# Order around seven norms rewritten, and two stages that scale their results by 1/rms instead of their inputs

## The chip, the cores and the metric

One Trainium2 chip, one of its cores. The metric is the device time of one launch, in microseconds (us), median over runs. TensorE multiplies (PE in the profile), VectorE (DVE), ScalarE (ACT) and GpSimd (POOL) do the elementwise work, SyncE (SP) starts the loads of weights. All five run at once and meet at semaphores.

## What is computed

A network of four layers on 512 tokens of width 1024, all in float32. The first half has two layers that end in layer norms, the second half two that use rms norms.

```
for layer in (0, 1):
    mix = hybrid_mixer(x) if layer == 0 else recurrent_mixer(x)
    x = layer_norm(DN_ALPHA * x + mix, ln1_g[layer], ln1_b[layer])
    x = layer_norm(DN_ALPHA * x + sqrelu_mlp(x, w1, w2), ln2_g[layer], ln2_b[layer])
h = x
for l in (0, 1):
    xn = rms_norm(h, g[0])
    mix = dilated_mixer(xn, w_qkv, w_o) if l == 0 else fox_mixer(xn, w_q, w_o, k, v, c)
    h = h + rms_norm(mix, g[1])
    h = h + rms_norm(conv_ffn(rms_norm(h, g[2]), w_up, conv, w_down), g[3])
rms_norm(x, g) = x * rsqrt(mean(x * x) + EPS) * g
```

`dilated_mixer` starts with q, k, v = xn @ w_qkv, then a rotation of q and k by position (rope) and banded attention. `fox_mixer` starts with q = xn @ w_q_b; its keys, values and gates come from rms_norm(h, kv_norm) @ w_kvf. So between every two matrix products stands a norm that needs a mean over the 1024 channels of each token before anything of the next product's input is final.

## The kernel before

Tokens lie along the free dimension (512), channels along the 128 partitions in 8 tiles (`X[:, m, :]`). A float32 product is done as three passes in a faster format: each operand is split in a high part and the rest (`XH`, `XL` for activations; `WH`, `WL` for weights), and `three` (L268 to L270) multiplies high by high, low by high and high by low. A **unit** is one 128-column block of a weight matrix times the whole input: 8 steps k of 3 matmuls, 24 in all. Unit u's weights are loaded to `RAW`, split by ScalarE (`split_hi`, L240) and VectorE (`split_lo`, L248), and lie in slot u % 4: a unit's weights can be split only when the unit four before it is done (`unit_done`).

Every engine runs its own list of instructions in the order in which the Python code issues it, and waits in it. That order is written by hand; the change rewrites it.

**At a norm** the tokens are worked in two halves, v = 0 and v = 1, of 256 columns. `last_four_pe` does the last four units of a stage, all of them for half 0 and then all for half 1, and between puts the two small matmuls of the statistics of half 0 (`stats_pe`, L443 for the sum and L447 for the sum of squares, with a matrix of 1/1024). `first_three_pe` does the first three units u0, u0+1, u0+2 of the next stage side by side, again half 0, then half 1: for each k it needs `XL[k]` of that half, and at k = 0 the split weights of the three. The statistics of half 1 go to TensorE behind its second step. The last four units occupy all four slots, so that the weights of u0 to u0+3 are split while the norm is computed. Meanwhile the others work per tile:

- layer norm: VectorE subtracts the mean (L498), GpSimd multiplies by 1/sigma (L512), ScalarE writes `XH` (L524) and `X` (L525) with gain and bias, VectorE writes `XL` (L504). `stats_end_act` and `stats_end_dve` turn the statistics into 1/sigma.
- rms norm of what is added (`rms_add_dve`): VectorE scales (L612) and adds (L615), GpSimd adds three of the eight tiles (L623), ScalarE writes `XH` (L651) and squares the new X (L539), GpSimd sums the squares (L553), VectorE writes `XL` (L642). Before the feed-forward stages 1/rms of the new X is applied to the results, since it is the same for all channels of a token.
- before the dilated and the query stage it is applied to the input: all squares of a half are summed, TensorE adds them over channels (`squares_pe`, L559), and only then VectorE writes x times gain times 1/rms (L582), ScalarE `XH` (L595) and VectorE `XL` (L587).

`lead_dve`, `lead_act` and `lead_pool` say between which tiles of half 0 the rest is done: results of half 1 taken from PSUM (`take`), its squares and sums (`stat`), and the splits of u0, u0+1 and u0+2, at tiles 3, 5 and 7.

There are eight such places: norms 0 to 2 (layer norms before `w1_0`, `rin`, `w1_1`), 3 (a layer norm and the rms norm before the dilated stage, `qkv`), 4 (`up_0`), 5 (the query stage, `wqb`), 6 (`up_1`) and 7 (the output).

Of the kernel before, what the change touches and what calls it, by code (L numbers as in the profile page):

```python
# [12 lines left out]
T = 512  # L13
# [120 lines left out]
def build_program(nc, D):  # L134
    with ExitStack() as ctx:
# [220 lines left out]
        HALF = (slice(0, 256), slice(256, 512))  # L356
        half_done = signal("half")
# [4 lines left out]
        def last_four_pe(pe, us, xh, xl, ready, taken, behind_first):  # L362

            kb = PLAN[us[4]][2]
            for v in range(2):
                for b, u in enumerate(us[4:8]):
                    claim(pe, b)
                    pe.wait_ge(w_lo, u)
                    for k in range(kb):
                        pe.wait_ge(*ready[k])  # L370
                        mm = three(pe, PS[b][:, HALF[v]], u, k, xh[k][:, HALF[v]], xl[k][:, HALF[v]], k == 0, k == kb - 1)
                    mm.then_inc(*(unit_done if v else half_done).at(u))
                    pe.until[b] = [taken(b + 4, v)]
                    if v and b == 0:
                        behind_first()
# [79 lines left out]
        def stats_end_act(act, n, v, mean):  # L455
# [6 lines left out]
            act.e.activation(S1[:, h], PS[b + 1][:, h], ACT.Square).then_inc(*st_m2.at((n, v)))  # L462
            act.wait_ge(st_var, (n, v))
            rstd_act(act, RS[:, h], S2[:, h], 1.0, EPS5, ("rstd", n, v)).then_inc(*st_r.at((n, v)))

        def stats_end_dve(dve, n, v):
# [9 lines left out]
              ("ln1", 1, ("rwo",), "mlp1"), ("ln2", 1, ("mlp", 1, 3), None)]  # L476
# [3 lines left out]
        BEFORE_STATS = {1: (st_r, (0, 1)), 2: (st_r, (1, 1)), 3: (st_r, (2, 1)), 4: (st_r, ("ln", 1)),  # L480
                        5: (st_r, (4, "x", 1)), 6: (st_r, (5, "x", 1)), 7: (st_r, (6, "x", 1))}
# [8 lines left out]

        def layer_norm_dve(dve, n, v, between):
            _, _, mix, stage = LN[n]
            h, b = HALF[v], 4 + 2 * v
            for i in range(10):
                if i < 8:
                    if i > 2:
                        dve.wait_ge(x_norm, (n, i - 3, v))
                    dve.e.tensor_tensor(TM[:, 3 + i % 3, h], X[:, i, h], PS[b + 1][:, h], ALU.subtract).then_inc(*ln_c.at((n, i, v)))  # L498
                m = i - 2
                if 0 < m and n == 3:  # L500
                    square_dve(dve, "ln", m, v)
# [13 lines left out]
        def layer_norm_act(act, n, v, between):  # L515
            name, l, _, stage = LN[n]
            h = HALF[v]
            for m in range(8):
# [7 lines left out]
                if n == 3:  # L526
                    act.wait_ge(x_norm, (n, m, v))
# [6 lines left out]
        def square_act(act, key, m, v):  # L534
            h, added = HALF[v], rs_sumd if key == "ln" else rs_sum
            if m > 2:
                act.wait_ge(added, (key, m - 2, v))
            out = TM[:, 6 + m % 2, h] if m else S1[:, h]
            act.e.activation(out, X[:, m, h], ACT.Square).then_inc(*rs_sq.at((key, m, v)))  # L539

        def square_dve(dve, key, m, v):
            h = HALF[v]
            dve.wait_ge(rs_sq, (key, m, v))
            if m > 1:
                dve.wait_ge(rs_sumd, (key, m - 1, v))
# [2549 lines left out]
```

## Time and profile before

| | |
|---|---|
| median of three runs | 2608.57 us (2605.19 to 2609.13) |
| profiled execution, own time | 2606.99 us |
| its span, first to last instruction | 2605.2 us |
| TensorE busy | 2457.0 us (94%) |
| VectorE busy | 1443.1 us (55%) |
| ScalarE busy | 1076.0 us (41%) |
| GpSimd busy | 304.1 us (12%) |
| granted clock of TensorE, mean | 0.969 |

The span is the time from the first to the last instruction in one profiled execution; 1.8 us lie around it. Busy shares are of the span. The granted clock is the share of TensorE's full speed; it takes two values, 1 and 0.5.

### The profile page before, as it was taken

To read this page: it belongs to the slowest core of one execution; us is meant where nothing else is said; L and a number is where in the kernel's file an instruction comes from. 1 tells how busy PE (TensorE), PEld (TensorE's weight loads), DVE (VectorE), ACT (ScalarE), POOL (GpSimd) and SP (SyncE) were. 2 spreads that over 40 slices of the span, in tenths; PEclk is the share of its full clock that TensorE was granted. 3 is DMA by queue.
4 is the path that set the end of the run, shared out by engine and by line. 5 is a ranking of instruction groups with operands and counts; after the bars stand their busy time and mean duration, and the time that the engine had idled before them with its cause. 6 is when DMAs were issued, how large, how long until landed. Compare 5 with 4: busy or idle time off the path is not lost.

```text
span 2605.2 us, 31632 instructions
## 1 busy us (share of the span) xinstructions
PE 2457.0 (94%) x12858; PEld 2029.9 (78%) x12858; DVE 1443.1 (55%) x2181; ACT 1076.0 (41%) x1878; POOL 304.1 (12%) x290
## 2 busy tenths in 40 slices
PE   8999989999989789999979979999979998999997
PEld 6768868888887688888857778888867777788886
DVE  6547755443366665334474467645475454676355
ACT  5533144232256554223254454433243555444332
POOL 0030130000031430000131021000020001101000
PEclk9989999999999899999989989999989999999998
DMA  5200012222213123222221123222212111232221
GB/s 196 89 33 1 17 43 88 101 93 97 97 50 113 65 76 103 97 97 97 81 78 57 41 69 110 97 97 94 84 64 91 33 49 50 81 109 86 98 100 45
DMA packets 56224, 206.47 MB, mean 79 GB/s; under 512 B 3680, under 2 KB 5776, under 8 KB 55952
## 3 DMA queue, kind: packets, MB, share of 16 engines
q1 hardware_dynamic: 55440, 201.34, 22.6%
q0 software_dynamic: 640, 3.12, 0.3%
q8 instruction: 102, 1.67, 0.3%
q14 instruction: 42, 0.34, 0.0%
HBM read 202.30 MB, written 2.10 MB: 78 GB/s over the span
## 4 chain that ended last, share of the span: by engine, by line
PE 80%; DVE 9%; issue 6%; ACT 4%; POOL 1%; DMA 0%; SPq 0%; POOLq 0%; DVEq 0%; ACTq 0%
PE ps L268 24%; PE ps L270 23%; PE ps L269 23%; DVE WL L248 2%; DVE TM L612 1%; ACT WH L240 1%; PE ps L317 1%; PE ps L2512 1%; PE ps L321 1%; PE ps L318 1%; PE ps L2541 1%; DVE X L615 1%; DVE AR L786 1%; DVE AR L1995 1%; DVE XL L642 1%
## 5 line engine op out<-in xcount | busy, mean ns | idle before, releaser
L268 PE MATMUL ps<-XH,WH 128*128 128x512 f32 (+1 forms) x2216 | 840.2, 379 | 92.2 <-DVE WL L248 39.3
L269 PE MATMUL ps<-XL,WH 128*128 128x512 f32 (+1 forms) x2216 | 819.2, 370 | 0.0
L270 PE MATMUL ps<-XH,WL 128*128 128x512 f32 (+1 forms) x2216 | 818.8, 369 | 0.0
L248 DVE TENSOR_TENSOR WL<-RAW,WH 128x1024 fp32r<-128x1024 f32 (+1 forms) x382 | 469.6, 1231 | 319.9 <-ACT WH L240 318.6
L268 PEld LDWEIGHTS ps<-XH,WH 128*128 128x128 f32 x2216 | 428.5, 193 | 181.4 <-issue 79.8
L240 ACT ACTIVATE WH<-RAW 128x1024 fp32r<-128x1024 f32 (+1 forms) x382 | 395.0, 1037 | 313.4 <-PE ps L270 305.7
L269 PEld LDWEIGHTS ps<-XL,WH 128*128 128x128 f32 x2216 | 428.9, 194 | 69.7 <-issue 4.6
L270 PEld LDWEIGHTS ps<-XH,WL 128*128 128x128 f32 x2216 | 427.9, 193 | 68.2
L268 PE MATMUL ps<-H,WH 128*128 128x512 f32 (+1 forms) x1104 | 405.5, 367 | 1.9 <-ACT AR L1903 1.9
L270 PE MATMUL ps<-H,WL 128*128 128x512 f32 (+1 forms) x1104 | 404.3, 366 | 0.0
L269 PE MATMUL ps<-H,WH 128*128 128x512 f32 (+1 forms) x1104 | 404.3, 366 | 0.0
L268 PEld LDWEIGHTS ps<-H,WH 128*128 128x128 f32 x1104 | 208.0, 188 | 40.2 <-DVE WL L248 2.3
L269 PEld LDWEIGHTS ps<-H,WH 128*128 128x128 f32 x1104 | 208.0, 188 | 37.6
L270 PEld LDWEIGHTS ps<-H,WL 128*128 128x128 f32 x1104 | 208.0, 188 | 37.4
L1176 ACT ACTIVATE TM<-TM,VEC 128x512 f32<-128x512 f32 x88 | 71.8, 816 | 209.1 <-DVE TM L1230 209.1
L1206 DVE SCALAR_TENSOR_TENSOR TM<-TM,VEC 128x511 f32<-128x511 f32 (+1 forms) x176 | 131.3, 746 | 3.1
L1273 POOL TENSOR_TENSOR TM<-TM 128x512 f32<-128x512 f32 x38 | 49.0, 1289 | 508.8 <-DVE TM L1206 468.1
L1075 DVE SCALAR_TENSOR_TENSOR TM<-ps,TM 128x512 f32<-128x512 f32 x64 | 44.2, 690 | 104.2 <-ACT TM L1054 104.2
L1054 ACT ACTIVATE TM<-ps 128x512 f32<-128x512 f32 x64 | 38.1, 595 | 136.9 <-PE ps L270 136.8
L1230 DVE TENSOR_TENSOR TM<-ps,TM 128x512 f32<-128x512 f32 x88 | 60.4, 687 | 40.1 <-PE ps L270 39.9
L623 POOL TENSOR_TENSOR X<-X,TM 128x256 f32<-128x256 f32 x24 | 23.2, 966 | 478.5 <-DVE TM L612 478.5
L420 DVE TENSOR_TENSOR TM<-TM 128x256 f32<-128x256 f32 (+1 forms) x88 | 55.5, 631 | 39.3 <-ACT TM L412 39.0
(369 smaller groups left out, 2535.6 us busy)
## 6 DMA issues: line engine op xcount, KB each, us to landing
RAW<-in_w SPq DMA_DIRECT2D x64, 1024.0 KB, 4.9
RAW<-in_up SPq DMA_DIRECT2D x44, 1024.0 KB, 4.9
RAW<-in_dn SPq DMA_DIRECT2D x16, 1024.0 KB, 4.9
RAW<-in_hyb SPq DMA_DIRECT2D x10, 1024.0 KB, 5.0
RAW<-in_qkv SPq DMA_DIRECT2D x9, 1024.0 KB, 4.8
RAW<-in_rin SPq DMA_DIRECT2D x8, 1024.0 KB, 4.8
RAW<-in_kvf SPq DMA_DIRECT2D x8, 1024.0 KB, 4.9
RAW<-in_dn SPq DMA_DIRECT2D x8, 768.0 KB, 4.4
```

The lines of the kernel that those rows point to most:

```text
L240: act.e.activation(WH[:, s, 0:n], RAW[:, g % NRAW, k, 0:n], ACT.Copy).then_inc(*w_hi.at(u))
L248: dve.e.tensor_tensor(WL[:, s, 0:n], RAW[:, g % NRAW, k, 0:n], f32(WH[:, s, 0:n]), ALU.subtract).then_inc(*w_lo.at(u))
L268: pe.e.matmul(out, wh, xh, start=first, stop=False)
L269: pe.e.matmul(out, wh, xl, start=False, stop=False)
L270: return pe.e.matmul(out, wl, xh, start=False, stop=last)
L420: dve.e.tensor_tensor(S2[:, c], S2[:, c], TM[:, 6 + m % 2, c], ALU.add).then_inc(*st_s2.at((n, m, v)))
L1054: act.e.activation(r, PS[m % 4][:, :], ACT.Relu).then_inc(*h_relu.at((l, q, m)))
L1075: dve.e.scalar_tensor_tensor(h, PS[m % 4][:, :], 0.0, r, ALU.max, ALU.mult).then_inc(*h_sq.at((l, q, m)))
L1176: act.e.activation(pair[s], TM[:, 6 + s, :], ACT.Identity, bias=vec("fcb", 44 * l + blk), scale=vec("fcw", 132 * l + 3 * blk + 2)).then_in ...
L1206: dve.e.scalar_tensor_tensor(dst[:, 2 - j:T], u[:, 0:T + j - 2], vec("fcw", 132 * l + 3 * blk + j), dst[:, 2 - j:T], ALU.mult, ALU.add).th ...
L1230: dve.e.tensor_tensor(TM[:, 6 + s, :], PS[b][:, :], RS, ALU.mult).then_inc(*f_u.at((l, q, m, s)))
L1273: pool.e.tensor_tensor(g, g, v, ALU.mult).then_inc(*gate_pool.at(("ffn", l, q, m)))
```

## The change

1. **The places in the order.** `lead_*` are gone. Each engine's list for half 0 is written out: results of half 1, weight splits and sums stand where their inputs are expected. ScalarE splits u0 before it computes 1/sigma, u0+1 behind tile 1, u0+2 behind tile 2, and now also u0+3 behind tile 7. VectorE subtracts the first means before it has the variance, and computes `XL` three tiles behind instead of two.
2. **TensorE.** The statistics of half 0 are issued behind step 5 of the first unit instead of behind its last step, those of half 1 behind step 2 of the next stage instead of step 1.
3. **Squares of the new X**, which were done for each half (256 columns), are done once at 512 columns, in half 1, and their matmul stands in unit 3 of the next stage (in unit 4 for `qkv`).
4. **Dilated stage.** `XH` and `XL` are made of x times gain alone. 1/rms (`RQ`) is multiplied into the sine and cosine tables of the rope; the values are scaled as they leave PSUM, five blocks by VectorE and the pair of token-major blocks by ScalarE with 1/rms as columns (four transposes). The ropes of the first three units wait for `RQ`; the attention steps start one unit later.
5. **Query stage.** The same; VectorE takes the results from PSUM with 1/rms and 1/8 (ScalarE did), in six banks instead of four.

```diff
-                    if v and b == 0:
-                        behind_first()
+                        if (v, b, k) == (1, 0, 5):
+                            behind_first()
...
+            def first(i):                      # norm_dve, half 0
+                if i == 2:
+                    stats_end_dve(dve, n, 0)
+                    take(4, 1)
+                    split_lo(dve, u0 + 1)
+                    stat(4, 1)
+                if i == 3:
+                    take(5, 1)
+                if i == 4:
+                    split_lo(dve, u0 + 2)
+                    stat(5, 1)
+                if i == 5:
+                    take(6, 1)
+                    split_lo(dve, u0 + 3)
+                if i == 6:
+                    stat(6, 1)
+                    take(7, 1)
+                    dve.wait_ge(x_mix, mixed(LN[n][2])(7, 1)[1])
+                    stat(7, 1)
+                if i == 10:
+                    split_lo(dve, u0 + 4)
...
+            def first(m):                      # norm_act, half 0
+                if m == 1:
+                    split_hi(act, u0 + 2)
+                    stat(5, 1)
+                if m == 2:
+                    split_hi(act, u0 + 3)
+                if m == 3:
+                    stat(6, 1)
+                    stat(7, 1)
+                if m == 7:
+                    split_hi(act, u0 + 4)
+
+            stats_end_act(act, n, 0, True, lambda: split_hi(act, u0 + 1))
+            stat(4, 1)
+            layer_norm_act(act, n, 0, first)
...
-                    square_act(act, "ln", m, v)
+                    act.e.activation(XH[:, m, h], X[:, m, h], ACT.Copy, scale=vec("ng", m)).then_inc(*x_hi.at(input_key(stage, m, v)))
...
+        def squares_pe(pe, key):
+            claim(pe, 4)
+            pe.wait_ge(rs_sumd if key == "ln" else rs_sum, (key, 7))
+            pe.e.matmul(PS[4][:, :], onesd, S1, start=True, stop=True).then_inc(*sq_sum.at(key))
...
+            def first_three():                 # dilated_in_dve, once 1/rms is there
+                dve.e.tensor_tensor(sin, sin, RQ, ALU.mult).then_inc(*dve_own.at("sin / rms"))
+                for j in range(3):
+                    rope_sin(j)
+                dve.e.tensor_tensor(rotated(what, jb), rotated(what, jb), c2("cos"), ALU.mult).then_inc(*rp_cosd.at(("dil", what, jb)))
+                for j in (0, 2, 1):
+                    rope_add(j)
...
-                act.e.activation(FQ[i], PS[i % 4][:, :], ACT.Copy, scale=0.125).then_inc(*ev_act.at(u))
+                dve.wait_ge(st_r, (5, "x"))
+                dve.e.scalar_tensor_tensor(FQ[i], PS[WQB_BANKS[i]][:, :], 0.125, RS, ALU.mult, ALU.mult).then_inc(*ev_dve.at(u))
```

On ScalarE, half 0 of norm 0 (L240 is a weight split; L412 a square of half 1; L451 and L453 make 1/sigma; L524, L525 `XH` and `X`) stood before as:

```order
L451 ACTIVATE TM<-TM,COL 128x256 [waits s_st_var]
L453 ACTIVATE TM<-TM 128x256 [waits s_act_own]
L524 ACTIVATE XH<-TM,VEC 128x256 [waits s_half,s_ln_p]
L525 ACTIVATE X<-TM,VEC 128x256
L524 ACTIVATE XH<-TM,VEC 128x256 [waits s_ln_p]
L525 ACTIVATE X<-TM,VEC 128x256
L524 ACTIVATE XH<-TM,VEC 128x256 [waits s_ln_p]
L525 ACTIVATE X<-TM,VEC 128x256
L412 ACTIVATE TM<-X 128x256 [waits s_x_mix]
L524 ACTIVATE XH<-TM,VEC 128x256 [waits s_ln_p]
L525 ACTIVATE X<-TM,VEC 128x256
L240 ACTIVATE WH<-RAW 128x1024 [waits s_unit,s_raw1]
```

and stands now as follows (L455 and L457 make 1/sigma, L416 squares, L535 and L536 are `XH` and `X`):

```order
L240 ACTIVATE WH<-RAW 128x1024 [waits s_unit,s_raw1]
L455 ACTIVATE TM<-TM,COL 128x256 [waits s_st_var]
L457 ACTIVATE TM<-TM 128x256 [waits s_act_own]
L416 ACTIVATE TM<-X 128x256 [waits s_x_mix]
L535 ACTIVATE XH<-TM,VEC 128x256 [waits s_half,s_ln_p]
L536 ACTIVATE X<-TM,VEC 128x256
L535 ACTIVATE XH<-TM,VEC 128x256 [waits s_ln_p]
L536 ACTIVATE X<-TM,VEC 128x256
L240 ACTIVATE WH<-RAW 128x1024 [waits s_unit]
L416 ACTIVATE TM<-X 128x256 [waits s_x_mix]
L535 ACTIVATE XH<-TM,VEC 128x256 [waits s_ln_p]
L536 ACTIVATE X<-TM,VEC 128x256
```

The split of u0 has moved from behind tile 3 to ahead of tile 0, that of u0+1 from behind tile 5 to behind tile 1.

On GpSimd, half 1 of norm 4 (L623 adds to X, L553 sums squares) stood before as:

```order
L623 TENSOR_TENSOR X<-X,TM 128x256 [waits s_ln_c]
L553 TENSOR_TENSOR TM<-TM 128x256 [waits s_rs_sq]
L553 TENSOR_TENSOR TM<-TM 128x256 [waits s_rs_sum,s_rs_sq]
L623 TENSOR_TENSOR X<-X,TM 128x256 [waits s_ln_c]
L553 TENSOR_TENSOR TM<-TM 128x256 [waits s_rs_sum,s_rs_sq] x2
L623 TENSOR_TENSOR X<-X,TM 128x256 [waits s_ln_c]
L553 TENSOR_TENSOR TM<-TM 128x256 [waits s_rs_sum,s_rs_sq] x3
```

and half 0 the same. Now both halves together (L604 adds, L566 sums squares) are:

```order
L604 TENSOR_TENSOR X<-X,TM 128x256 [waits s_ln_c] x4
L566 TENSOR_TENSOR TM<-TM 128x512 [waits s_rs_sq]
L566 TENSOR_TENSOR TM<-TM 128x512 [waits s_rs_sum,s_rs_sq]
L604 TENSOR_TENSOR X<-X,TM 128x256 [waits s_ln_c]
L566 TENSOR_TENSOR TM<-TM 128x512 [waits s_rs_sum,s_rs_sq] x2
L604 TENSOR_TENSOR X<-X,TM 128x256 [waits s_ln_c]
L566 TENSOR_TENSOR TM<-TM 128x512 [waits s_rs_sum,s_rs_sq] x3
```

Half 0 has lost its seven sums, and the seven of half 1 are twice as wide.

On TensorE, the step from the last layer's product to the dilated stage stood before as:

```order
L268 MATMUL ps<-H,WH 128x256
L269 MATMUL ps<-H,WH 128x256
L270 MATMUL ps<-H,WL 128x256
L559 MATMUL ps<-TM,CST 128x256 [waits s_rs_sumd,s_st_var]
L443 MATMUL ps<-TM,CST 128x256 [waits s_st_s1d,s_ln_c]
L447 MATMUL ps<-TM,CST 128x256 [waits s_st_s2]
L268 MATMUL ps<-XH,WH 128x256 [waits s_x_lo,s_w_lo,s_x_mix]
```

Now the sum of squares (L571) stands in unit 4 of that stage, ahead of the first rope matmul (L839):

```order
L270 MATMUL ps<-XH,WL 128x512
L571 MATMUL ps<-TM,CST 128x512 [waits s_rs_sumd,s_st_var]
L268 MATMUL ps<-XH,WH 128x512
L269 MATMUL ps<-XL,WH 128x512
L270 MATMUL ps<-XH,WL 128x512
L839 MATMUL ps<-AR,CST 128x512 [waits s_st_var]
```

The wait for the sums of squares no longer stands between the two stages.

## Rows read from the trace of the kernel before

**Rows 1.** Waits of TensorE over the span: us in total, times, longest
```profile
PE ps L268 <- DVE WL L248: 39.3, 14, 4.3
...
PE ps L559 <- POOL TM L553: 13.5, 2, 8.4
PE ps L559 <- DVE TM L546: 12.7, 2, 7.2
...
PE ps L268 <- issue: 11.3, 5, 4.8
PE ps L268 <- DVE XL L587: 8.3, 4, 2.7
...
PE ps L447 <- DVE TM L420: 4.4, 1, 4.4
```

**Rows 2.** Windows: stretch, length, busy (x) of PE PEld DVE ACT POOL, clock, DMA
```profile
357.50:411.57 54.07, 46.04 (x345) 44.74 (x344) 35.15 (x65) 29.88 (x56) 22.88 (x25) 0.91 0.18 61
...
1283.43:1349.08 65.65, 49.19 (x350) 46.62 (x349) 43.59 (x91) 34.55 (x73) 20.28 (x24) 0.84 0.17 60
1501.19:1556.10 54.91, 40.49 (x297) 38.92 (x296) 36.97 (x59) 29.29 (x65) 17.79 (x20) 0.88 0.16 58
1886.10:1946.16 60.06, 42.04 (x298) 39.97 (x297) 43.80 (x81) 24.66 (x55) 17.49 (x21) 0.80 0.15 53
2182.19:2240.39 58.20, 44.81 (x345) 43.33 (x344) 36.47 (x58) 29.16 (x64) 17.77 (x20) 0.91 0.14 50
```

**Rows 3.** Timeline of TensorE at norm 0: start, length, [idle before <- by]
```profile
372.40 0.28 PE L270 MATMUL ps<-XH,WL 128*128 128x256 f32 x1
372.52 0.70 PE L443 MATMUL ps<-TM,CST 128*128 128x256 f32 x2
373.06 0.59 PE L447 MATMUL ps<-TM,CST 128*128 128x256 f32 x2
...
383.49 0.36 PE L268 MATMUL ps<-XH,WH 128*128 128x256 f32 x1 [1.22 <-issue]
...
387.62 0.55 PE L268 MATMUL ps<-XH,WH 128*128 128x256 f32 x1 [3.53 <-DVE WL L248]
...
391.47 0.55 PE L268 MATMUL ps<-XH,WH 128*128 128x256 f32 x1 [2.88 <-DVE WL L248]
```

**Rows 4.** Groups of VectorE, half 0 of norm 0: xcount | busy us, mean ns | idle before
```profile
L248 DVE TENSOR_TENSOR WL<-RAW,WH 128x1024 fp32r<-128x1024 f32 x3 | 4.6, 1533 | 0.1
L504 DVE TENSOR_TENSOR XL<-X,XH 128x256 fp32r<-128x256 f32 x8 | 4.4, 547 | 2.2 <-ACT X L525 2.0
L498 DVE TENSOR_TENSOR TM<-X,ps 128x256 f32<-128x256 f32 x8 | 3.1, 410 | 0.0
```

**Rows 5.** Groups of ScalarE in the same stretch
```profile
L524 ACT ACTIVATE XH<-TM,VEC 128x256 fp32r<-128x256 f32 x8 | 4.7, 593 | 1.1 <-POOL TM L512 0.9
...
L240 ACT ACTIVATE WH<-RAW 128x1024 fp32r<-128x1024 f32 x3 | 3.1, 1042 | 0.0
```

**Rows 6.** Timeline of VectorE, half 1 of norm 0: first and last XL
```profile
399.90 0.51 DVE L504 TENSOR_TENSOR XL<-X,XH 128x256 fp32r<-128x256 f32 x1 [2.05 <-ACT X L525]
...
407.45 0.42 DVE L504 TENSOR_TENSOR XL<-X,XH 128x256 fp32r<-128x256 f32 x1 [0.78 <-ACT X L525]
```

**Rows 7.** Timeline at norm 4: VectorE alone, then beside GpSimd
```profile
1514.09 0.42 DVE L615 TENSOR_TENSOR X<-X,TM 128x256 f32<-128x256 f32 x1
...
1539.86 0.91 POOL L553 TENSOR_TENSOR TM<-TM 128x256 f32<-128x256 f32 x1
...
1540.21 0.84 DVE L615 TENSOR_TENSOR X<-X,TM 128x256 f32<-128x256 f32 x1
```

**Rows 8.** Group of GpSimd, 345 to 352: a sum at 512 columns
```profile
L1776 POOL TENSOR_TENSOR TM<-TM,AR 128x512 f32<-128x512 f32 x1 | 1.3, 1289 | 2.1 <-DVE TM L1741 2.1
```

**Rows 9.** Timeline of TensorE, first full unit behind norm 4
```profile
1556.10 0.47 PE L268 MATMUL ps<-XH,WH 128*128 128x512 f32 x1 [3.31 <-DVE WL L248]
```

**Rows 10.** Window in the dilated stage, columns as in rows 2
```profile
1350.00:1400.00 50.00, 48.24 (x232) 33.39 (x231) 27.93 (x37) 21.39 (x57) 11.09 (x8) 1.00 0.24 79
```

More of the change, by code:

```diff
@@ L721, in norm_act, with norm_pool, first @@
             layer_norm_act(act, n, 1, nothing)
             if n == 3:
[L723 to L726 removed]
+                for m in range(8):
+                    square_act(act, "ln", m)
+        def norm_pool(pool, n, then=None):
             def stat(m, v):
[L728 to L729 removed]
+                stat_pool(pool, n, m, v, X[:, m, :], mixed(LN[n][2])(m, v))
+            def first(i):
+                if i == 0:
+                    stat(4, 1)
+                if i == 2:
+                    stat(5, 1)
+                if i == 4:
+                    stat(6, 1)
+            layer_norm_pool(pool, n, 0, first)
+            if then:
+                then()
@@ L2155, in dil_steps_pe @@
                 if d == 6:
[L2156 removed]
+                    for _ in range(4):
                         yield
@@ L2213, in dilated_in_pe, with ROT_BANK, norm_columns_pe @@
                     pe.until[banks[0]] = [(rp_in, key)]
-                    rope_mid.append((key, rotated(what, jb), cst["rot2"]))
+                    rope_mid.append((key, rotated(what, jb), cst["rot2"], ROT_BANK(i)))
             run(steps)
+        def ROT_BANK(i):
+            return (6, 5, 7)[i] if i < 3 else 6
+        def norm_columns_pe(pe):
+            claim(pe, 6)
+            pe.wait_ge(st_r, ("ln", "x"))
+            for t in range(4):
+                mm = pe.e.transpose(PS[6][:, 128 * t:128 * t + 128], RQ[:, 128 * t:128 * t + 128], ident)
+            mm.then_inc(*nm_col.at(0))
+            pe.until[6] = [(act_own, "1/rms columns")]
+        nm_col, rp_cosd = signal("nm_col"), signal("rp_cosd")
         def turn_values_pe(pe, jb):
@@ L2235, in v_pair_act, with scaled_pair_act @@
             v.then_inc(*ev_act.at(us[1]))
+        def scaled_pair_act(act, dst, us, banks):
+            act.wait_ge(unit_done, us[1])
+            act.wait_ge(act_own, "1/rms columns")
+            if us[0] % NW > us[1] % NW:
+                dst = dst[::-1]
+            for t in range(4):
+                src = PS[banks[t // 2]][:, :].rearrange("p (t n c) -> p t n c", t=2, n=2)
+                for n in range(2):
+                    v = act.e.activation(dst[n][:, 128 * t:128 * t + 128], src[:, t % 2, n, :], ACT.Copy, scale=RC[:, t:t + 1])
+            v.then_inc(*ev_act.at(us[1]))
         def dil_exp_act(act, d):
```

525 lines of the change are left out of this document (271 added, 254 removed).

## The prediction

> **What bounds the kernel now.** I read the page, then the waits of TensorE, then its clock and idle time window by window. TensorE is busy over 90% of the span, so a change off its path is worth nothing, and the question is what becomes of its idle time. The waits [rows 1] are to be read by what ends them. The largest, 39.3 us in 14 waits, is for the low part of a split weight (L248), not for a norm. With it goes "issue", 11.3 us in 5: at norm 0 the wait marked so ends right after a split too. Then come 13.5 and 12.7 us for the sums of squares of the new X before the `wqb` and `qkv` stages (L559), 8.3 us for `XL` there (L587), and 4.4 us at the last norm.
>
> The windows [rows 2] run from the first half-width matmul at a norm to the first full-width one behind it. Length less busy time is TensorE's idle time: 8.0 us at norm 0 (norms 1 and 2 look alike), 16.5 at norm 3, 14.4 at norm 4, 18.0 at norm 5 and 13.4 at norm 6; with 4.4 at norm 7 that is 91 us. The clock column is the second loss: 0.91 to 0.80, where the clock fell from 1 to 0.5 in a long idle and stayed down when work resumed. Its price: norm 0 holds 336 matmuls that follow each other at 0.12 us [rows 3], 40.3 us, and four small ones at some 0.6, so 42.6; busy were 46.0, hence 3.4 us of slow clock. Reckoned alike it is about 5 at norm 3, 2.5 at norm 4, 3.5 at norm 5, 1 at norm 6: 22 us with three times norm 0. So 113 us are there to be had, and no more.
>
> Why the weights are late: the splits of u0, u0+1 and u0+2 stand behind tiles 3, 5 and 7 of half 0. At norm 0 TensorE was through with the last four units at 382.27 (383.49 less 1.22), ran three matmuls, waited to 387.62 for u0+1 and to 391.47 for u0+2 [rows 3].
>
> **The change, part by part.** I walk the new order of each engine, with durations of rows, each instruction starting when its engine is free and its inputs are there.
>
> *Norms 0 to 2.* The statistics of half 0 end at 373.65 at norm 0 [rows 3]. The first unit is done three quarters of a microsecond later than before, since they now stand ahead of its last 6 matmuls (which wait for a sum that came at 372.5); ScalarE splits u0 (1.04 [rows 5]) at 374.2, so 1/sigma comes 1 us later than before. VectorE has u0 at 377.0, u0+1 at 382.4 and u0+2 at 385.4: between the last two stand a square's sum, a subtraction and an `XL` (about 0.4 each, up to 0.55 [rows 4]), and a split takes 1.5 beside GpSimd instead of 1.2. TensorE comes at 383.0: it waits 2 us for u0+2 where it waited 7.6. The last tile's square of half 1 waits for its `take`, which VectorE reaches only at 386.7; ScalarE stands until then, and has the remaining four tiles (two passes of 0.5 us each, by the spacing behind the 0.59 [rows 5]), and a fourth split, to do: half 0 is through at 391.6 on VectorE and 392.0 on ScalarE. TensorE is through with its half 0 at 394.6; before it was so at 402.9 (411.57 less 72 matmuls of 0.12).
>
> What is late next is half 1 of the norm itself. Its 1/sigma starts only now; the first `XL` came 400.4 before [rows 6] and comes at 398.8 by the walk. TensorE waits 4.2 us. From there the norm's pace, 7.5 us for eight tiles [rows 6], is a little faster than TensorE's 8.6 (72 times 0.12), so it ends at 407.5 if the clock stays up, before 411.6: gain 4.1. A wait of 4 us is of the length behind which the clock fell elsewhere; some 5 us at half speed cost 2.5: gain 1.6. I take the middle, 2.8, at norms 0 and 2, and 3.5 at norm 1, whose sums are ready when TensorE comes by earlier. **Norms 0 to 2: 9 us** (5 to 13; bounds 0, if the norm keeps its old pace in half 1, and 34, all that is lost there).
>
> *Norm 3.* The two waits for squares and all that hung on them leave the path; what remains is a layer norm like norm 0, whose `XH` and `XL` are a little dearer (gain multiply, 1 us in all). Norm 0's walk gives a window of 50 us (54.07 less 4.1), or 52.5 with a slow clock, and 1 more here, where it was 65.65 [rows 2]: 12 to 15; its sums are ready when TensorE comes, as at norm 1, which puts me at the upper end, 15. Behind it stand ropes that wait for 1/rms: the squares (8 on ScalarE, 7 sums on VectorE at 512 columns) lie beside unit 3, the tables and three ropes on VectorE (8 operations of 0.7, 5.6 us) beside units 4 and 5, for which ScalarE has filled other banks. VectorE is busy 27.9 of 50 us there [rows 10], so the cover is good; without it up to 5.6 us come back. I take 1 us for it: **14 us**.
>
> *Norm 4.* In half 0 the weights are early as above: waits of 1.2 and 1.3 us instead of 11. GpSimd has no sums there any more, which frees VectorE, because the two hamper each other: an addition takes 0.42 alone and 0.84 beside a GpSimd sum of 0.91 [rows 7]. In half 1 that comes back: seven sums take 1.29 each [rows 8] instead of 0.91, 2.7 us, with start-ups some 3.5 us more for VectorE. By the walk half 1 ends at 1547.7, where 1556.1 was [rows 9]. Its last wait, 3.3 us for the split of u0+3 [rows 9], which stood behind 1/rms, is gone, but the split of u0+4 now stands in that place: squares at step 5 of unit 3, then two ScalarE passes (0.75 each, an estimate at twice the columns of the 0.5 us passes), the high split (1.0) and the low one (1.2), 3.7 us, of which the last 6 matmuls of unit 3 cover 1.4: with the semaphores 2.5 us of waiting. **6 us.**
>
> *Norm 6* is the same with 8 steps a unit, which hide a little more: **6.5**. *Norm 5* loses the 13.5 us of waits for squares and its half of the 8.3 for `XL` [rows 1], against new waits of 3.3 for weights and 2 ahead of half 1; half 1 ends about 12.5 us earlier, and the same 2.5 us at unit 4 come back. VectorE has 8 more evacuations of 0.7 in the query stage, hidden by units of over 5 us (24 matmuls of twice some 0.12) of which its other work takes some 2: **10**. *Norm 7*: sums of half 1 are ready about 1 us sooner: **1**.
>
> Here the Trainium skill has a rule (SBUF — State Buffer, section "SBUF: two separate sides"): a VectorE instruction with two SBUF inputs and a GpSimd instruction share a port pair as an exclusive lock, and the loser waits for the whole instruction. Our rows agree as to the single instruction. By the rule alone the half 1 of norms 4 to 6 would grow by all of the added GpSimd time and its start-ups, as rival A has it.
>
> **The sum.** 9 + 14 + 6 + 10 + 6.5 + 1 = 46.5 us. The profiled execution took 2606.99 us by its own time, which gives 2560.5; the median of the runs is 1.6 higher, so I forecast 2562.
>
> **The rivals.**
> A, *the norm is the bound.* VectorE and ScalarE can't give more in half 0 for all that is put into it, and GpSimd's wide sums stop VectorE fully in half 1: VectorE's 21 operations of about 0.42 (8.8 us) and GpSimd's three of 0.91 and seven of 1.29 (11.8) in a row are 20.6 us, some 3 more than I took, at three norms. For it: VectorE is idle only 2.3 us in half 0 of norm 0 [rows 4]. With norms 0 to 2 at nothing and 3 less at norm 3: 46.5 - 9 - 9 - 3, a gain of 25: 2583.
> B, *my waits are too long.* Where half 1's first `XL` comes in time, the clock stays up too: norms 0 to 3 give some 6 us more each: a gain of 68, 2540. Against it: ScalarE stands 2 us for the last `take` in the walk, by the order.
> C, *the dilated stage gives some back.* Ropes, columns and scaled values hang on 1/rms, the attention steps start a unit later; if the 5.6 us of first ropes and 1 us in each of ten later units show, less the 1 I took: 2562 + 14.6 = 2577.
> D, *slower.* One mechanism: rope i on VectorE frees the one bank in which TensorE turns i + 1, and every unit of the dilated stage waits for it. VectorE is idle 22 of 50 us there [rows 10], so all of that must be filled before it holds anyone, and it decides from 46.5 us of waiting on, 3.3 us in each of 14 units; new are 5.6 us at the first units and 0.7 in five. At twice that point, 6.6 us a unit, it would be 2655.
> E, *no change*: the gains at norms cancel against C and A together: 2608.
>
> **How the numbers follow.** Forecast 0.52 (2547 to 2573: norms 0 to 2 from 5 to 13, norm 3 from 11 to 16, norms 4 to 6 from 17 to 27), A 0.16, B 0.13, C 0.13, D 0.03, E 0.03. The range 2543 to 2583 leaves out D, E and the far ends of A and B. Faster by over 0.2% (5.2 us, about what this kernel's measurement can tell): 0.95. Within: 0.02. Slower: 0.03.
>
> **What the profile after would show.** Waits for L248 fall from 39.3 us to below 20, and those that are left stand one at u0+2 and one at unit 4 behind norms 4 to 6. L559's successor, the wide sum of squares, has no wait above 1 us. The windows: about 51 us for norms 0 to 2, 50 for norm 3, 47 for norm 4, 48 for norm 5. The new, longest kind of wait is for `XL` at the first step of half 1, 3 to 5 us at norms 0 to 3, with a clock that falls at some of them. The forecast is wrong if that wait is absent (B), if the windows of norms 0 to 2 keep 54 us (A), or if TensorE idles over 3 us in the dilated stage for ropes (C).

## The result, and the profile after

The changed kernel takes 2577.06 us, median of four runs (2576.22 to 2579.68), beside 2607.72 us of the kernel before on the same chip: ratio 0.9885, 95% interval 0.9868 to 0.9902. That is 30.7 us where 46.5 were forecast. The time lies in the predicted range, near rival C's 2577, though for other reasons than C's.

The profiled execution was the slowest of the four (2579.68 us, span 2577.8), so between the two profiled spans lie 27.4 us, and these are what is shared out below. From the page:

```profile
span 2577.8 us, 31473 instructions
...
PE 2461.8 (95%) x12854; PEld 2033.3 (79%) x12854; DVE 1438.7 (56%) x2156; ACT 1065.5 (41%) x1831; POOL 300.4 (12%) x269
```

The mean granted clock is 0.977. TensorE's waits, as in [rows 1] (us in total, times, longest):

```profile
PE ps L268 <- DVE WL L248: 21.2, 13, 2.3
PE ps L268 <- DVE XL L619: 18.3, 14, 2.4
...
PE ps L268 <- DVE XL L512: 11.1, 3, 4.1
...
PE ps L268 <- DVE XL L514: 3.5, 1, 3.5
PE ps L451 <- DVE TM L424: 2.8, 1, 2.8
```

The waits for squares ahead of the dilated and the query stage are gone, and the wide matmul (L571) waits nowhere. Waits for weights fell from 39.3 to 21.2 us, a little short of the "below 20" that was expected. Two kinds are new: `XL` at the first step of half 1 of norms 0 to 3 (L512, L514), as predicted, and `XL` within the halves of norms 4 to 6 (L619, 18.3 us in 14; 0.8 us once before), which was not. The windows, as in [rows 2], for norms 0, 2, 3, 4, 5 and 6:

```profile
358.34:410.94 52.60, 46.08 (x346) 44.91 (x345) 34.59 (x65) 29.66 (x56) 23.32 (x25) 0.94 0.24 81
910.00:963.75 53.75, 45.74 (x346) 44.63 (x344) 34.61 (x65) 29.68 (x56) 23.39 (x25) 0.94 0.24 79
1278.98:1329.91 50.93, 45.13 (x345) 44.55 (x344) 34.50 (x65) 30.40 (x58) 21.47 (x24) 0.93 0.24 80
1483.01:1532.28 49.27, 41.40 (x293) 39.92 (x292) 37.26 (x58) 25.16 (x52) 15.19 (x13) 0.90 0.24 85
1867.25:1917.79 50.54, 41.84 (x293) 39.45 (x292) 38.60 (x65) 21.93 (x42) 15.94 (x14) 0.90 0.18 63
2159.04:2211.25 52.21, 45.59 (x342) 44.03 (x341) 36.84 (x57) 25.37 (x51) 15.19 (x13) 0.93 0.22 77
```

Norm 3 lost 14.7 us of its window. Norm 2 lost 0.3 and norm 0 only 1.5, and of its 52.60 us TensorE is still busy 46.1, where some 42.6 would do at full clock, by the prediction's reckoning. The remaining 3.5 us of slow clock are what they were before. Three places of TensorE's timeline (start, length, [idle before]) and the window behind the third:

```profile
386.70 0.35 PE L268 MATMUL ps<-XH,WH 128*128 128x256 f32 x1 [2.10 <-DVE WL L248]
...
400.72 0.38 PE L268 MATMUL ps<-XH,WH 128*128 128x256 f32 x1 [3.41 <-DVE XL L512]
...
1541.05 0.50 PE L268 MATMUL ps<-XH,WH 128*128 128x512 f32 x1 [2.28 <-DVE WL L248]
```
```profile
1541.05:1546.00 4.95, 4.95 (x15) 3.92 (x16) 3.09 (x5) 2.48 (x3) 0.00 (x0) 0.66 0.08 7
```

These are the waits that the walk named: 2 us for u0+2, 4.2 at half 1, 2.5 at unit 4. Behind the last the clock was 0.66 for 4.95 us, 1.7 us lost on top of the 2.28.

Last, VectorE in half 1 of norm 4 (L596 adds to X, L619 is `XL`), and GpSimd beside it (L566 is the wide sum):

```profile
1515.41 1.39 DVE L596 TENSOR_TENSOR X<-X,TM 128x256 f32<-128x256 f32 x1
1516.72 1.49 DVE L619 SCALAR_TENSOR_TENSOR XL<-X,VEC,XH 128x256 fp32r<-128x256 f32 x1
...
1518.53 0.47 DVE L619 SCALAR_TENSOR_TENSOR XL<-X,VEC,XH 128x256 fp32r<-128x256 f32 x1
...
1519.91 1.40 DVE L596 TENSOR_TENSOR X<-X,TM 128x256 f32<-128x256 f32 x1
1521.23 1.50 DVE L619 SCALAR_TENSOR_TENSOR XL<-X,VEC,XH 128x256 fp32r<-128x256 f32 x1
```
```profile
1514.18 0.91 POOL L604 TENSOR_TENSOR X<-X,TM 128x256 f32<-128x256 f32 x1 [5.68 <-DVE TM L593]
1515.05 2.88 POOL L566 TENSOR_TENSOR TM<-TM 128x512 f32<-128x512 f32 x2
```

An addition that takes 0.42 us alone takes 1.40 beside a wide sum, and `XL` 1.50 instead of 0.47. The long ones end 0.28 to 0.29 us behind the end of a GpSimd instruction: that of 1516.72 at 1518.21, the sums at 1517.93.

### The profile page after: what moved, and what is told of

Same layout as the page of the kernel before. It is cut to its first block, busy times and chain, and to the rows that moved or that the text cites. A ratio compares the mean times of both kernels' runs of the same rounds, so it can differ in the third digit from the quotient of the medians.

```text
span 2577.8 us, 31473 instructions
## 1 busy us (share of the span) xinstructions
PE 2461.8 (95%) x12854; PEld 2033.3 (79%) x12854; DVE 1438.7 (56%) x2156; ACT 1065.5 (41%) x1831; POOL 300.4 (12%) x269
## 4 chain that ended last, share of the span: by engine, by line
PE 79%; DVE 10%; issue 5%; ACT 4%; POOL 1%; DMA 0%; SPq 0%; DVEq 0%; POOLq 0%; ACTq 0%
PE ps L268 23%; PE ps L270 23%; PE ps L269 23%; DVE WL L248 2%; DVE TM L593 1%; ACT WH L240 1%; DVE TM L424 1%; PE ps L317 1%; DVE XL L619 1%; PE ps L2598 1%; DVE X L596 1%; PE ps L321 1%; PE ps L318 1%; PE ps L2627 1%; DVE AR L781 1%
## 5 line engine op out<-in xcount | busy, mean ns | idle before, releaser
L268 PE MATMUL ps<-XH,WH 128*128 128x512 f32 (+1 forms) x2216 | 844.8, 381 | 86.1 <-DVE WL L248 21.2
L248 DVE TENSOR_TENSOR WL<-RAW,WH 128x1024 fp32r<-128x1024 f32 (+1 forms) x382 | 465.9, 1221 | 325.9 <-ACT WH L240 325.1
L240 ACT ACTIVATE WH<-RAW 128x1024 fp32r<-128x1024 f32 (+1 forms) x382 | 395.2, 1038 | 326.9 <-PE ps L270 319.5
L424 DVE TENSOR_TENSOR TM<-TM 128x256 f32<-128x256 f32 (+1 forms) x88 | 61.1, 694 | 41.4 <-ACT TM L416 41.1
L604 POOL TENSOR_TENSOR X<-X,TM 128x256 f32<-128x256 f32 x24 | 23.0, 960 | 484.5 <-DVE TM L593 484.5
```

The costliest lines, as they stand in the source:

```text
L240: act.e.activation(WH[:, s, 0:n], RAW[:, g % NRAW, k, 0:n], ACT.Copy).then_inc(*w_hi.at(u))
L248: dve.e.tensor_tensor(WL[:, s, 0:n], RAW[:, g % NRAW, k, 0:n], f32(WH[:, s, 0:n]), ALU.subtract).then_inc(*w_lo.at(u))
L268: pe.e.matmul(out, wh, xh, start=first, stop=False)
L424: dve.e.tensor_tensor(S2[:, c], S2[:, c], TM[:, 6 + m % 2, c], ALU.add).then_inc(*st_s2.at((n, m, v)))
```

## Experiments

All are the changed kernel with one edit each unless said otherwise, with four or five runs each. Ratios are to the kernel before, run beside them; differences between variants are differences of medians. The runs of one variant spread by 0.6 to 6.6 us, and the median of the kernel before moved between 2606.89 and 2608.17 us from group to group, so a difference of about 1 us between variants says nothing. In the code the second argument of `split_hi` and `split_lo` is a bound: `split_hi(act, u0 + 5)` splits the units up to u0+4.

**Late sums.** At norms 4 to 6:

```diff
-                if v:
-                    square_act(act, n, m)
                 between(m)
+            if v:
+                for m in range(8):
+                    square_act(act, n, m)
...
             rms_add_dve(dve, n, v, gi, low)
+            if v:
+                for m in range(1, 8):
+                    square_dve(dve, n, m)
```

GpSimd's seven `square_pool` are gone.

> The changed kernel, with one thing altered at norms 4, 5 and 6: the squares and their wide sums come behind half 1, and VectorE makes the sums instead of GpSimd. Theory (GpSimd's seven wide sums stop VectorE in half 1): in the changed kernel three additions of VectorE there take 1.40 us instead of 0.42 and four low parts 1.50 instead of 0.48, 7 us in all. Without the sums half 1 takes VectorE 9.8 us instead of 17.2; TensorE's waits there (5.7 us at norm 4) and the slow clock behind them go, 5 to 8 us a norm: 2557 us (2552 to 2563). Rival (VectorE has too much to do wherever the sums stand, and the wait moves to the wide matmul): a gain of 0 to 5, 2572 to 2577, with a wait above 3 us at the wide matmul.

Measured: 2555.40 us, ratio 0.98 (0.9787 to 0.9813), 21.7 us less than the changed kernel. The first three rows are norms 4, 5 and 6. The last is VectorE's half 1 of norm 4 from its first scaling to its last `XL`; the same stretch of the changed kernel stands below it:

```profile
1484.08:1525.67 41.59, 38.34 (x293) 37.06 (x292) 32.17 (x61) 23.95 (x49) 6.13 (x6) 0.96 0.28 101
1859.96:1902.21 42.25, 38.01 (x294) 36.81 (x292) 34.56 (x68) 20.60 (x39) 6.54 (x7) 0.96 0.22 75
2143.38:2187.71 44.33, 42.24 (x341) 40.96 (x340) 31.77 (x60) 24.13 (x48) 6.14 (x6) 1.00 0.25 90
...
1512.92:1523.08 10.16, 9.04 (x70) 8.23 (x69) 9.99 (x22) 4.71 (x10) 2.73 (x3) 1.00 0.29 103
```
```profile
1511.91:1529.06 17.15, 11.49 (x74) 10.46 (x73) 16.97 (x22) 8.12 (x16) 12.11 (x10) 0.88 0.17 61
```

The same 21 operations of VectorE (x22 counts the end of a split too) take 10.2 us instead of 17.2, and the windows shrink by 7.7, 8.3 and 7.9. Three additions and four `XL` that are 1.0 us shorter each make up the 7. ScalarE's squares moved as well, but VectorE had been busy for 16.97 of the 17.15 us, so it was not ScalarE that it waited for. The wide matmul has no wait. The theory holds.

One thing came along that the edit does not explain. TensorE's wait at unit 4 behind norm 4 is 2.27 us, as in the changed kernel (2.28), but the clock behind it stayed at 1.00, where it had been 0.66:

```profile
1534.46 0.50 PE L268 MATMUL ps<-XH,WH 128*128 128x512 f32 x1 [2.27 <-DVE WL L248]
```
```profile
1534.46:1539.46 5.00, 5.00 (x22) 4.16 (x23) 3.13 (x5) 2.52 (x4) 0.00 (x0) 1.00 0.09 13
```

**GpSimd late.** The same edit, but the seven sums stay on GpSimd (`square_pool` behind `rms_add_pool`).

> The changed kernel, with the squares of the new X and their wide sums behind half 1 at norms 4, 5 and 6, but still made by GpSimd (the run with late sums had them on VectorE). Theory (what cost time in half 1 is that the sums run beside VectorE, not that GpSimd makes them): the windows are as short as with VectorE's late sums (41.6, 42.3 and 44.3 us), no operation of VectorE in half 1 takes over 1 us, but seven sums of 1.29 us with 0.14 between them are 10 us and the wide matmul waits about 3 us for the last, with a slow clock behind it of 1.7: some 4.7 us more than that run at each norm, 2555.4 plus 14, 2569.5 us (2565 to 2574). Rival (it was the squares and sums as such, in whichever queue): the windows stay at 48 us or more and the time at 2577.

Measured: 2570.25 us, ratio 0.9859 (0.9846 to 0.9873). Norm 4's window and the wide matmul:

```profile
1481.05:1522.69 41.64, 38.33 (x294) 37.06 (x292) 30.26 (x58) 23.31 (x48) 7.77 (x8) 0.96 0.29 101
```
```profile
1530.56 1.19 PE L571 MATMUL ps<-TM,CST 128*128 128x512 f32 x1 [3.60 <-POOL TM L566]
```

The window is as short as with VectorE's sums, so the place of the sums cost the time, not the engine that makes them. The engine costs the wait behind: 3.6 us at each of the three norms (10.8 in all). With the slow clock that follows, the up_0 stage is 5.5 us longer (339.80 us, 334.29 with VectorE's sums).

**Narrow sums.** The squares of norms 4 to 6 per half again:

```diff
-                if v:
-                    square_act(act, n, m)
+                square_half_act(act, n, m, v)
...
-            pool.e.tensor_tensor(S1, S1, TM[:, 6 + m % 2, :], ALU.add).then_inc(*rs_sum.at((key, m)))
+            pool.e.tensor_tensor(S1[:, h], S1[:, h], TM[:, 6 + m % 2, h], ALU.add).then_inc(*rs_sum.at((key, m, v)))
```

> The changed kernel, with the squares of the new X at norms 4, 5 and 6 done again for each half at 256 columns, on ScalarE and GpSimd as before the change; one wide matmul adds them over the channels as in the changed kernel. Theory (each GpSimd sum holds VectorE for its own length): half 1 loses 7 times 0.38 us of sums, 2.7 us, and half 0 gets seven sums of 0.91 us, 6.4 us, of which about half meets VectorE at work: 0 to 2 us slower a norm, 2580 us (2575 to 2584). Rival (the sums cost VectorE in half 1 only by their width): 3 us a norm come back, 2568.

Measured: 2570.10 us, ratio 0.9851 (0.9834 to 0.9867), 7.0 us faster than the changed kernel. Norm 4, and VectorE's half 1 of it:

```profile
1484.76:1532.08 47.32, 39.59 (x293) 38.19 (x292) 36.75 (x58) 26.01 (x60) 17.91 (x20) 0.93 0.25 88
...
1516.65:1529.96 13.31, 8.80 (x67) 7.99 (x67) 13.14 (x22) 6.53 (x16) 8.48 (x10) 1.00 0.20 79
```
```profile
1523.55 0.84 DVE L604 TENSOR_TENSOR X<-X,TM 128x256 f32<-128x256 f32 x1
```

The rival was right. In half 1 VectorE took 3.8 us less, since an addition now takes 0.84 instead of 1.40. In half 0, where seven sums stand again, norm 4's waits for u0+1 and u0+2 are 1.80 and 1.41 us instead of 1.33 and 0.88: one us. Squaring once at 512 columns made the kernel slower than squaring twice at 256.

**Split ahead.** At norms 4 to 6:

```diff
             rms_add_on_act(act, n, 1, nothing)
+            split_hi(act, u0 + 5)
             squares_end_act(act, n)
```

> The changed kernel, with the high part of u0+4 split by ScalarE ahead of 1/rms of the new X instead of behind it, at norms 4, 5 and 6. Theory (the wait of 2.28 us at unit 4 costs a slow clock behind it as well): the up_0 stage grew from 330.0 to 335.0 us, of which 0.4 is the wide matmul; 4.5 us come back at each of three norms, 13.5 in all: 2563.5 us. Rival (only the wait itself comes back, the longer stage has another cause): 6.8 us, 2570.

Measured: 2569.51 us, ratio 0.9856 (0.9843 to 0.987), 7.5 us: the rival's number, but not its reason. The first row below is the stretch that holds the start of unit 4, the second the whole stage up to norm 5, 334.97 us in the changed kernel:

```profile
1534.00:1539.00 5.00, 5.00 (x22) 3.80 (x21) 0.69 (x1) 2.64 (x4) 0.00 (x0) 1.00 0.00 0
1530.32:1862.61 332.29, 331.06 (x1444) 270.88 (x1443) 191.12 (x233) 130.71 (x166) 24.48 (x19) 1.00 0.28 95
```
```profile
1554.38 0.47 PE L268 MATMUL ps<-XH,WH 128*128 128x512 f32 x1 [1.23 <-DVE WL L248]
```

The wait and the slow clock are both gone, 2.28 and 1.68 us, but 1.23 came back at unit 7, whose split stood behind evacuations (results taken out of PSUM) that wait for 1/rms: 2.7 us net.

**Both splits.** `split_ahead`, and the split of u0+7 in the feed-forward stages one evacuation earlier (`split_for(..., 4)` instead of 3).

> The changed kernel with the split of u0+4 ahead of 1/rms as in the run before, and besides the split of u0+7 in the two feed-forward stages one evacuation earlier on ScalarE and VectorE. In that run the wait of 2.28 us at unit 4 was gone and TensorE's clock stayed at 1.00 where it had been 0.66 for 5 us, but a wait of 1.24 us for the split of u0+7 stood at unit 7 of both feed-forward stages. Theory (that wait is all that kept 3 times 4 us from coming back): 2.5 us less than the 2569.5 of that run, 2567. Rival (the evacuations that wait for 1/rms are the limit, the wait moves on to a later unit): no less than 2569.

Measured: 2569.91 us, ratio 0.9852 (0.9838 to 0.9867), no gain by the median. (The kernel before was 1.3 us slower in this group; reckoned against it, the gain is 0.9 us.) The trace tells why:

```profile
1533.58:1864.81 331.23, 331.06 (x1445) 270.89 (x1444) 190.92 (x233) 130.68 (x166) 24.50 (x19) 1.00 0.29 96
1864.81:1915.49 50.68, 41.50 (x293) 39.12 (x292) 38.60 (x65) 22.75 (x43) 15.93 (x14) 0.90 0.18 63
```

The wait at unit 7 is gone and did not move on: the stage is 1.06 us shorter, and the other one 1.03. But norm 5's window, which this edit doesn't touch, was 50.68 us, where the run before had 48.73. Neither theory foresaw that. It is the clock, not the order; see the last section.

**Half 1 ahead.** At norms 0 to 3, on VectorE (ScalarE alike):

```diff
-                if i == 10:
-                    split_lo(dve, u0 + 4)
-
-            def second(i):
-                if i == 2:
-                    stats_end_dve(dve, n, 1)
-
             layer_norm_dve(dve, n, 0, first)
-            layer_norm_dve(dve, n, 1, second)
+            stats_end_dve(dve, n, 1)
+            layer_norm_dve(dve, n, 1, nothing)
+            split_lo(dve, u0 + 4)
```

> The changed kernel, with the split of u0+3 behind half 1 of norms 0 to 3 on ScalarE and VectorE, and the variance of half 1 ahead of the three subtractions. Theory (the 3.4 to 4.1 us wait for XL at the first step of half 1 is made by what stands ahead of 1/sigma: a split of 1.04 on ScalarE, one of 1.22 and three subtractions of 0.33 on VectorE): the first XL of half 1 comes 2.6 us sooner, the wait falls to about 1 us and the clock stays up: 4 us at each of four norms, 2561 us. Rival (the end of half 0 on ScalarE sets it, and only its own 1.04 us split counts): 1 us a norm, 2573.

Measured: 2561.96 us, ratio 0.9828 (0.9815 to 0.9841), 15.1 us. Norms 0, 2 and 3, and the wait at half 1 of norm 0:

```profile
358.16:406.63 48.47, 44.52 (x346) 43.43 (x344) 34.56 (x65) 29.68 (x56) 23.33 (x25) 0.96 0.18 66
...
902.94:951.50 48.56, 43.20 (x345) 42.09 (x344) 34.60 (x65) 29.70 (x56) 23.40 (x25) 1.00 0.19 66
1266.73:1314.04 47.31, 42.66 (x345) 41.70 (x344) 32.70 (x62) 28.99 (x55) 21.49 (x24) 1.00 0.17 63
```
```profile
397.89 0.39 PE L268 MATMUL ps<-XH,WH 128*128 128x256 f32 x1 [0.84 <-DVE XL L512]
```

The wait fell by 2.57 us at norm 0, as expected to the tenth, and the window by 4.13. The rest is clock: at norm 2 the wait fell by 2.65 (4.14 to 1.49), the window by 5.19, and the clock rose from 0.94 to 1.00. The theory holds.

**Old places.** The splits, results and sums of norms 0 to 3 where `lead_*` had them, and `XL` two tiles behind; scaling and all else as changed.

> The changed kernel, with the old places of splits, results of half 1 and sums at norms 0 to 3 (as before the change), and all else kept, the scaling behind the dilated stage too. Theory (at norm 3 the gain is that of the two waits for squares, and the places give there what they give at norms 0 to 2): windows of norms 0 to 2 at 54 us again, norm 3 at 54.5: 7 to 8 us slower than the changed kernel, 2585 us. Rival (the places carry most of norm 3): norm 3 at 60 us or more, 2591.

Measured: 2589.49 us, ratio 0.9931 (0.9919 to 0.9944), 12.4 us slower than the changed kernel. Norm 3 up to the first full-width matmul, and that matmul:

```profile
1285.48:1344.34 58.86, 45.53 (x345) 44.40 (x344) 37.13 (x69) 33.82 (x63) 21.12 (x24) 0.89 0.14 51
```
```profile
1344.34 0.77 PE L268 MATMUL ps<-XH,WH 128*128 128x512 f32 x1 [5.57 <-DVE WL L248]
```

Norm 0's window is 52.79 us, as good as in the changed kernel (52.60), and norm 2's 53.99 (53.75): at these two the new places alone gave nothing. TensorE waited 3.5 and 2.9 us for weights there, where the changed kernel waits 2.1 for weights and 3.4 for `XL` at half 1. At norm 1 they gave 3.4 us (54.40 to 50.96), and 2.0 more in the stage behind it.

At norm 3 the window is 58.86 us where it was 65.65 before and is 50.93 now. So 6.8 of its 14.7 us come with the old places too, from the scaling, and 7.9 only with the new ones. Of these, 5.57 are the wait at its end, which neither theory had: the split of u0+3 then stands behind the eight squares. The window lies between the theory's 54.5 and the rival's 60, nearer the rival, and so does the time: the places carry about half of norm 3.

**Statistics back.** TensorE issues the statistics of half 0 behind the first unit again.

> The changed kernel, with the statistics of half 0 issued by TensorE behind the last step of the first unit again, at all eight norms. Theory (1/sigma of half 0 starts a norm, and what is late there is the splits and passes that hang on it): the 0.6 us waits for the sums at norms 0 and 2 go, but all of half 0 comes 0.6 us later and so does the wait for u0+2: 0 to 1 us slower a norm, 2581 us (2577 to 2585). Rival (only the waits of 0.6 us count): 1 to 2 us faster, 2575.5.

Measured: 2576.44 us, ratio 0.9877 (0.9863 to 0.9892), the same as the changed kernel. The 0.6 us waits went, those for u0+2 grew by as little (2.10 to 2.41 at norm 0). The theory's 2581 did not come, and the rival's 2575.5 can't be told from no change: in total this part of the change does nothing. It does move time from norm to norm: norm 2's window was 51.15 us (53.75 in the changed kernel), norm 3's 52.50 (50.93).

**All together.** Late sums on VectorE, both splits, half 1 ahead, and at norms 0 to 3 the split of u0+2 and `take(7)` one operation earlier.

> The changed kernel with all the edits together: sums of squares behind half 1 on VectorE, the splits of u0+4 and u0+7 early, 1/sigma of half 1 ahead of the split of u0+3 at norms 0 to 3, and there also the split of u0+2 and the last result of half 1 one operation earlier on VectorE. Theory (the causes are apart from each other, their gains add): 21.7, 15.1 and 7.5 us as measured alone, 2.5 for the split of u0+7, and 5 for the two earlier operations: 2577 less 52, 2525 us (2518 to 2532). Rival (they overlap, since the same sums and splits stand in one queue): 2535 or more.

Measured: 2531.94 us, ratio 0.9708 (0.9693 to 0.9722), 45.1 us faster than the changed kernel and about 76 than the kernel before. The three edits alone add to 44.3; what was expected of the rest (7.5 us) hardly came. Norms 0 and 4:

```profile
360.12:407.90 47.78, 43.28 (x345) 42.09 (x344) 34.89 (x65) 29.66 (x56) 22.43 (x25) 1.00 0.19 67
...
1469.30:1511.72 42.42, 38.35 (x293) 36.95 (x292) 32.90 (x62) 24.55 (x50) 5.79 (x6) 0.96 0.29 99
```

**Finer.** `take(6, 1)` ahead of the split of u0+2 as well, and the sum of squares behind it.

> The kernel with all the edits together, and at norms 0 to 3 the result of unit 6 taken ahead of the split of u0+2 on VectorE, and the sum of squares behind it. In the run with all edits TensorE waited 2.0 us there at the third unit, and what came at that moment was not a split but the taking of a result out of the bank that this unit writes to, at 388.31. Theory (the bank is what is late): TensorE comes back 1 us sooner at four norms and the slow clock behind it is shorter: 4 to 6 us less than 2531.9, 2527 us. Rival (half 0 is VectorE's in full, what is moved forward pushes the sums of half 1 back by as much, and the wait for XL at half 1 takes it): 2532, within 1.5.

Measured: 2530.24 us, ratio 0.9706 (0.9693 to 0.9719), against 0.9708: no difference that these runs can tell. TensorE came back 0.5 us sooner (the wait is 1.47 instead of 2.01) and lost it at the sums (0.82 instead of 0.41) and at `XL` of half 1 (1.41 instead of 1.09). The rival holds: VectorE's half 0 there is full.

## Why the prediction was right in direction and its gain half as large again as the measured one

Between the profiled spans, by windows and by the stages between them (forecast, measured): norms 0 to 2, 9 and 4.4; norm 3, 14 and 13.8; norms 4 to 6, 22.5 and 7.6; norm 7, 1 and 1.7. Together 46.5 and 27.4. The time lies in the stated range, but that owes something to the width of the range: the forecast gave each part bounds of its own, and only norm 3 lies inside (11 to 16). Norms 0 to 2 were to give 5 to 13, norms 4 to 6 17 to 27. (These bounds, with norm 7, add to 2552 to 2575, not to the 2547 to 2573 that stand beside them.)

- *The walk.* It put TensorE's waits at norm 0 at 2 and 4.2 us and at unit 4 at 2.5; they are 2.10, 3.41 and 2.28. Half 1 of norm 4 was to cost VectorE 3.5 us more; it took 17.15 us where the narrow sums took 13.31. The order was read rightly.
- *Norms 0 to 2.* The failed step is "I take the middle, 2.8": it weighed a slow clock behind the wait at half 1 as half likely, and gave none to the 2 us wait for u0+2. At norm 0 both had one: 3.5 us, as before the change. At norm 2 the clock stayed at 1.00 behind the wait of 2.12 us and was 0.50 for 5 us behind that of 4.14. Norm 2 also had two waits of some 0.65 us at the statistics that the walk had missed. And 0.8 us were lost ahead of norm 0, where nothing was changed: that stretch took 356.6 to 360.1 us in the twelve traces. The experiment with half 1 ahead shows wait and clock leaving together.
- *Norm 3.* 14.7 in the window, 1.0 given back in the dilated stage (152.1 to 153.1 us): the term was 15 minus 1. That the 14 came out is right for the two causes together; that the scaling alone gave 6.8 of the window and the places 7.9, the forecast didn't separate. Rival C, whose time came out, is false: TensorE idles 2.4 us in that stage, 2.7 before.
- *Norms 4 to 6, half 1.* 5.6, 9.5 and 6.0 us where 8.4, 12.5 and 9 were taken. At norm 4 the last `XL` came 46.05 us behind the start of the window, within 0.7 us of the walk, which had TensorE through at 46.5 with a step of 1.1 behind it. But TensorE was through only at 49.27: it had waited 0.5, 2.4, 0.7 and 2.1 us in a row for `XL`, and did its last two steps in 3.2 us, where 2.1 do at full clock. The failed step is "by the walk half 1 ends at 1547.7", which took VectorE's pace for TensorE's and left the clock at 1. Late sums price the whole mechanism, GpSimd's sums beside VectorE in half 1, at 21.7 us for three norms. The forecast had charged 3.5 a norm for the widening alone, and for that it was enough: the narrow sums gave back 7.0 us in all. The rest was there with the narrow sums of the kernel before as well, and the walk, at VectorE's pace, had no wait of TensorE for it.
- *Norms 4 to 6, unit 4.* 2.5 us were taken for each; the up_0 stage grew by 4.97: the wait of 2.28, slow clock 1.68 behind it, and 0.87 for the wide matmul, which stands in this stage now (from its start at 1536.38 to the second matmul behind it are 1.09 us, where one matmul takes 0.23; the two narrow ones stood in the window before). The failed step is that these 2.5 us held the wait alone. In the query stage it was 5.2. Before norm 7 it was 3.4: there a slow clock had already stood in the stage before the change (331.61 us of work against 330.00 in up_0).
- *Rival A* had its mechanism half right. GpSimd's sums do stop VectorE until they end, and half 0 of norms 0 to 2 is full. But VectorE's price was 3.8 us at norm 4, near the 3.5 taken and not A's 6.5; norms 0 to 2 gave 4.4 us instead of nothing (only norm 2 kept nearly its 54 us, A's sign) and norm 3 nearly its full 14. What pushed norms 4 to 6 below even A's number (13.5 us; 7.6 came) was for the most part the clock: at norm 4 it cost 1.1 us in the last two steps and 1.7 at unit 4, beside 0.9 for the wide matmul and a step of TensorE's that was still to do behind the last `XL`.
- *"GpSimd has no sums there any more, which frees VectorE"* was over-valued: half 0 gained one us by it, VectorE's half 1 lost 3.8.

What stays open: the 4.5 us that TensorE still idles at norm 0 with all edits together, for which VectorE's half 0 would have to lose work, and why the clock falls behind a wait in one trace and not behind the same wait in another.

## What to carry to other kernels

Walk the order by hand, as here, let TensorE walk at its own pace behind the norm's, and then charge every wait of TensorE of 2 us and more, such as those here, with a chance of a slow clock behind it. Where the slow clock went with the wait, 1.5 to 2 times the wait came back (4.13 for 2.57 us, 5.19 for 2.65, 3.96 for 2.28). It is a chance and no rule: behind 2.27 us at unit 4 the clock stayed up in the run with late sums. A sum on GpSimd should lie where VectorE has nothing to do, however idle GpSimd is; if it can't, narrow pieces cost less than wide ones (7.0 us less here, with twice as many). Compare stretches up to the same instruction, or a wait at the border is lost from the account. Ahead of a value on which a whole half hangs, nothing should stand that is needed only behind that half: moving one unit's split behind it, and three subtractions behind the variance, gave 15 us at four norms.

## What the runs showed of the hardware

- VectorE beside GpSimd: the price goes by the length of GpSimd's instruction. One addition takes 0.42 us alone, 0.84 beside sums of 0.91 and 1.40 beside sums of 1.29. The long ones at norm 4 end 0.28 to 0.29 us behind the end of the sum, wherever in it they began: so VectorE waits until the GpSimd instruction under way is over. Operations that read one input from PSUM are not touched: two of them (L506 and L992) amid GpSimd's work at norm 0 took 0.41 each, while a sum of two SBUF inputs (L424) took 0.96. It works the other way too: GpSimd's L440, begun at 385.50 beside a split of VectorE (L248, 385.35 to 386.56), took 1.65, where the one at 380.84 took 0.75.

```profile
386.48 0.41 DVE L506 TENSOR_TENSOR TM<-X,ps 128x256 f32<-128x256 f32 x1
386.81 0.62 DVE L512 TENSOR_TENSOR XL<-X,XH 128x256 fp32r<-128x256 f32 x1
387.36 0.96 DVE L424 TENSOR_TENSOR TM<-TM 128x256 f32<-128x256 f32 x1
388.23 0.41 DVE L992 SCALAR_TENSOR_TENSOR X<-X,ps 128x256 f32<-128x256 f32 x1
```
```profile
385.50 1.65 POOL L440 TENSOR_TENSOR TM<-TM,X 128x256 f32<-128x256 f32 x1 [1.36 <-DVE X L992]
387.11 1.80 POOL L523 TENSOR_TENSOR TM<-TM 128x256 f32<-128x256 f32 x2
```

  The Trainium skill (SBUF — State Buffer, section "SBUF: two separate sides") has it that the port pair which GpSimd shares with VectorE's operations of two SBUF inputs is an exclusive lock, held for a whole instruction by whoever starts first. These rows agree, and the late sums put its price here at 21.7 us.
- One order of instructions does not have one time, and here the clock is the reason. Norm 5's window, in six kernels with the same order up to its last `XL`, was 50.54 and 50.68 us in two traces and 48.73, 48.25, 48.85 and 48.23 in four. VectorE and GpSimd did the same in all six: the last `XL` came 45.6 to 45.7 us behind the start of the window. What differs is TensorE's clock behind it. From 42.64 us behind the start to the end of the window, in the changed kernel and in the one with half 1 ahead, the same 36 matmuls of TensorE took 7.35 and 4.65 us, at 0.57 and 1.00 of the clock:

```profile
1909.89:1917.79 7.90, 7.35 (x36) 7.05 (x37) 2.98 (x5) 1.03 (x2) 2.51 (x3) 0.57 0.00 1
```
```profile
1895.14:1900.75 5.61, 4.65 (x36) 4.45 (x37) 2.99 (x5) 1.03 (x2) 2.53 (x3) 1.00 0.00 1
```

  A difference of 2 us in one trace is no verdict there.
- Waits of 2.1 to 2.3 us can be enough for the clock to fall from 1 to 0.5 behind them (norm 0, unit 4), but need not be: it stayed at 1.00 behind 2.12 us at norm 2, and behind 2.27 at unit 4 with late sums. The kernel before had a wait of 3.31 us ahead of its up_0 stage [rows 9], and in the 4.90 us behind it the clock was 1.00.
